# The output projection of a two-layer encoder step done by seven products of block sums, as the quad ahead of the MLP

## The reference

```python
    n = rms_norm(x, ln1_w)
    proj = n @ w_in
    q, k, v, g, gate_b, gate_c, hc = jnp.split(proj, SPLITS, axis=-1)
    ...
    ret_out = (jax.nn.silu(g.astype(jnp.float32)) * o).astype(x.dtype)
    ...
    conv_out = gate_b * z
    ...
    x = x + jnp.concatenate([ret_out, conv_out], axis=-1) @ w_out

    h2 = rms_norm(x, ln2_w)
    x = x + jnp.square(jax.nn.relu(h2 @ w_up)) @ w_down
```

## Time and profile before

| | us |
|---|---|
| median of 3 runs | 1404.87 (1402.94 to 1405.62) |
| the profiled execution, its own time | 1403.99 |
| its span, first to last instruction | 1402.0 |
| PE busy | 1381.7 (99%) |
| DVE busy | 897.2 (64%) |
| ACT busy | 594.9 (42%) |
| POOL busy | 166.0 (12%) |

### The profile page before, as it was taken

How to read it: one execution, slowest core, us unless ns; L and a number is a source line. 1 busy time by engine, 2 the same in 40 slices (tenths; PEclk the granted TensorE clock), 3 DMA queues, 4 the chain that set the end, 5 groups by cost and what they waited for, 6 DMA issues and landing times.

```text
span 1402.0 us, 21312 instructions
## 1 busy us (share of the span) xinstructions
PE 1381.7 (99%) x7750; PEld 1242.3 (89%) x7750; DVE 897.2 (64%) x1104; ACT 594.9 (42%) x712; POOL 166.0 (12%) x185
## 2 busy tenths in 40 slices
PE   8999999999999999999999999999999999999997
PEld 6888999889889899899878889998898998998986
DVE  6336515269976867868861474262788678688586
ACT  5211222157636446446533012231584464464563
POOL 2343200010000000000033431000100000000001
PEclk9999999999999999999999999999999999999999
DMA  7424212126454645455142242113345454544623
GB/s 274 136 76 122 83 50 73 55 105 156 88 153 121 150 98 149 140 116 159 31 134 102 91 121 68 61 62 120 76 129 142 110 158 124 121 121 121 151 61 105
DMA packets 91614, 158.18 MB, mean 113 GB/s; under 512 B 3892, under 2 KB 21428, under 8 KB 91512
## 3 DMA queue, kind: packets, MB, share of 16 engines
q1 hardware_dynamic: 74472, 123.18, 26.1%
q0 software_dynamic: 16896, 33.56, 14.1%
q10 hardware_dynamic: 144, 0.07, 0.0%
HBM read 149.38 MB, written 7.41 MB: 112 GB/s over the span
## 4 chain that ended last, share of the span: by engine, by line
PE 95%; DVE 1%; issue 1%; ACT 1%; DMA 0%; POOL 0%; SPq 0%; DVEq 0%; POOLq 0%; ACTq 0%
PE pair L776 27%; PE pair L615 23%; PE pair L832 21%; PE pair L625 12%; PE pair L845 6%; PE pair L665 2%; PE pair L703 1%; PE pair L710 1%; PE pair L684 1%; PE pair L688 1%; PE pair L693 1%; DMA w_raw<-in_w_in 0%; PE pair L696 0%; DVE ring L1738 0%; DVE x L1784 0%
## 5 line engine op out<-in xcount | busy, mean ns | idle before, releaser
L776 PE MATMUL pair<-mlp_in_hi,ring 128*128 128x320 f32 x1728 | 381.5, 309 | 0.0
L1104 ACT ACTIVATE ring<-raws 128x1024 fp32r<-128x1024 f32 x220 | 230.9, 1058 | 250.0 <-PE pair L832 129.8
L1738 DVE TENSOR_TENSOR ring<-raws,ring 128x1024 fp32r<-128x1024 f32 x220 | 267.1, 1221 | 103.0 <-ACT ring L1104 101.6
L832 PE MATMUL pair<-ring,a_ring 128*128 128x512 f32 x1344 | 312.1, 390 | 0.0
L832 PEld LDWEIGHTS pair<-ring,a_ring 128*128 128x128 f32 x1344 | 251.9, 188 | 52.5
L776 PEld LDWEIGHTS pair<-mlp_in_hi,ring 128*128 128x128 f32 x1728 | 289.1, 188 | 0.2
L776 PE MATMUL pair<-mlp_in_lo,ring 128*128 128x320 f32 x864 | 266.8, 309 | 0.0
L776 PEld LDWEIGHTS pair<-mlp_in_lo,ring 128*128 128x128 f32 x864 | 162.1, 188 | 0.2
L625 PE MATMUL pair<-norm_hi,ring 128*128 128x320 f32 x512 | 114.5, 310 | 0.0
L615 PE MATMUL pair<-ring,norm_hi 128*128 128x512 f32 x320 | 100.5, 395 | 2.7 <-DVE norm_lo L1502 2.6
L615 PE MATMUL pair<-pair_a,norm_hi 128*128 128x512 f32 x320 | 100.9, 397 | 0.0
(11 more groups left out here) (161 smaller groups left out, 1943.9 us busy)
## 6 DMA issues: line engine op xcount, KB each, us to landing
raws<-in_w_mlp_up SPq DMA_DIRECT2D x32, 1024.0 KB, 5.5
raws<-in_w_mlp_down SPq DMA_DIRECT2D x32, 1024.0 KB, 5.1
w_raw<-in_w_in SPq DMA_DIRECT2D x27, 1024.0 KB, 6.0
raws<-in_w_mlp_up POOLq DMA_DIRECT2D x16, 1024.0 KB, 9.0
raws<-in_w_mlp_down POOLq DMA_DIRECT2D x16, 1024.0 KB, 8.8
w_raw<-in_w_out SPq DMA_DIRECT2D x8, 1024.0 KB, 5.1
past_state<-in_state_ret SPq DMA_DIRECT2D x8, 512.0 KB, 4.4
out_ret_s<-past_state SPq DMA_DIRECT2D x8, 512.0 KB, 4.9
```

What stands on the lines that cost most here:

```text
L776: mm = pe.matmul(out[:, n, 0:HALF], item_half(item, h, a)[:, k, n * P:(n + 1) * P], mlp_in[i][c][:, k], start=(i in (B11, B21, SUM_1112, B ...
L832: mm = pe.matmul(out[:], a_item[:, a, 2 * h + k, pair * P:(pair + 1) * P], item_half(item, h, c)[:, k], start=(i in (B11, B21, SUM_1112) a ...
L1104: nc.scalar.activation(item_half(item, h, 0), raw_half(quad, RAW_OF[i], h), ACT.Copy).then_inc(half_hi.sem, 1)
L1738: nc.vector.tensor_tensor(item_half(item, h, 1), raw_half(quad, RAW_OF[i], h), f(item_half(item, h, 0)), ALU.subtract).then_inc(half_lo.se ...
```

## The change

O leaves the table of groups. The output projection becomes a down quad of its own, block number `OUT = -1`, ahead of the first MLP block: seven products with the four quarters of `w_out`, plus the sample's four. Its activations are the unsplit outputs in `hidden` (retention in the first half, z times B in the second), and `a_item_hi`, `a_item_lo`, `a_difference`, `mid_hi_of` and `sample_lo` split and sum them as in every down quad. All quads are numbered one higher. The transposes for the MLP's norm now stand between the pieces of that quad's last product (three tiles) and inside and behind the second half of the first up product (two tiles). The order of the tiles is the sample, then 0 to 3, and in the up quads the sample stands between the token halves (`MLP_PLACE`), so that tiles 0 and 1 and half of the sample make the first half. The squares go to a place of their own. Of the three input differences, two move to POOL.

```diff
-OUT_ORDER = [0, 1, 2, 3, SAMPLE]
+
+MLP_PLACE = {0: 0, 1: 1, SAMPLE: 2, 2: 3, 3: 4}
...
-          + [(s, ft, h) for s in "CHB" for ft in range(FT) for h in range(2)]
-          + [("O", dh, t) for dh in range(2) for t in OUT_ORDER])
+          + [(s, ft, h) for s in "CHB" for ft in range(FT) for h in range(2)])
...
-QUADS = 2 * NBLK
+QUADS = 2 * NBLK + 1
+OUT = -1
...
-                units(7, for_w_out, 0)
-                units(8, for_w_out, 1)
-
+                sp.wait_ge(group_done.sem, group_done.at(layer, STAGE_START[6]))
+                settle(sp)
+                for name in ("11", "12", "21", "22"):
+                    load_quarter(layer, 0, name)
...
+                            if b == 0 and i == B11 and h == 1:
+                                up_half(b, i, h, lambda: turn_tile(3))
+                                turn_tile(4)
+                            else:
+                                up_half(b, i, h)
...
+                                if b == OUT and i == SUM_ALL and (h, pair) != (1, 1):
+                                    turn_tile(2 * h + pair)
...
+                down(OUT)
                 for b in range(NBLK):
                     up(b)
                     down(b)
...
+                    if quad == 0:
+                        for t in range(NT):
+                            row_rstd(layer, NT, t)
+
+                        last = TURN["n2", NT - 1, 1]
+                        pool.wait_ge(turn_lo.sem, turn_lo.at(layer, split_turns_to(last)))
+                        nc.gpsimd.tensor_tensor(s2_raw[:], t_diff[:], t11[:], ALU.subtract).then_inc(s2_ready.sem, 1)
+                        nc.gpsimd.tensor_tensor(t21[:], t11[:], t21[:], ALU.subtract).then_inc(s3_ready.sem, 1)
...
                 def up(b):
-                    q, item = 2 * b, 2 * b * PRODUCTS
-                    if b:
-                        for p in range(2):
-                            add_to_x(b - 1, SUM_ALL, p)
-                    else:
-                        weight_half(1, 0)
+                    q, item = 2 * b + 1, up_item(b, 0)
+                    for p in range(2):
+                        add_to_x(b - 1, SUM_ALL, p)
+                    if b == 0:
+                        weight_half(item, 1)
+                        normalise(layer, NT, 3, ORDER[3], 32)
+                        normalise(layer, NT, 4, ORDER[4], 32)
+                        weight_half(item + 1, 0)
+                        read_turn_lo(layer, ("n2", 3, 1))
+                        weight_half(item + 1, 1)
+                        read_turn_lo(layer, ("n2", 4, 1))
                         weight_sum(q, SUM_1112, 0)
-                    weight_half(item + 1, 1)
-                    if b == 0:
+                        in_diff_lo_of(0)
+                        weight_half(item + 2, 0)
+                        hidden_sum(b, B21, 0)
                         weight_sum(q, SUM_1112, 1)
-                        read_turn_lo(layer, ("n2", NT - 2, 1))
-                    weight_half(item + 2, 0)
-                    if b == 0:
-                        read_turn_lo(layer, ("n2", NT - 1, 1))
-                    weight_sum(q, SUM_111222, 0)
-                    if b == 0:
-                        in_diff_lo_of(0)
-                        hidden_sum(b, B21, 0)
-                        in_difference(1)
+                        hidden_sum(b, B21, 1)
                         weight_half(item + 2, 1)
-                        hidden_sum(b, B21, 1)
-                        weight_sum(q, SUM_111222, 1)
+                        weight_sum(q, SUM_111222, 0)
                         in_diff_lo_of(1)
                         weight_half(item + 3, 0)
-                        in_difference(0)
+                        weight_sum(q, SUM_111222, 1)
...
+                    if b == OUT:
+                        add_to_x(b, B22, 0)
+                        normalise(layer, NT, 0, ORDER[0], 32)
+                        add_to_x(b, B22, 1)
+                        weight_half(item + 7, 0)
+                        normalise(layer, NT, 1, ORDER[1], 32)
+                        read_tile_lo(0)
+                        normalise(layer, NT, 2, ORDER[2], 32)
+                        read_tile_lo(1)
+                        read_tile_lo(2)
+                        return
```

More of the change, by code:

```diff
@@ L72 @@
 TURN = {x: n for n, x in enumerate(TURNS)}
[L73 to L74 removed]
+SPLIT_TURNS = [n for n, x in enumerate(TURNS) if x[0] == "n1"
+               or (x[0] == "n2" and (ORDER[x[1]] not in (2, 3) or x[2] == 1))]
 def split_turns_to(n):
@@ L317, in n2_parts @@
         def n2_parts(tile):
-            first = tile * P
+            first = MLP_PLACE[tile] * P
             out = []
@@ L773, in up_half @@
                     for n in range(2):
+                        if n and between:
+                            between()
                         for k in range(4):
@@ L812, in wait_banks, with turn_tile @@
                             layer, b * len(C_SUMS) + C_SUMS.index((read, h)) + 1))
+                def turn_tile(p):
+                    for c in range(2):
+                        turn(layer, ("n2", p, c))
                 def up(b):
@@ L907, in square @@
             def square(layer, base, p, tile):
-                if p >= 2:
-                    turns = TURN["n1" if base == 0 else "n2", p - 2, 1]
-                    act.wait_ge(turned.sem, turned.at(layer, turns + 1))
-                nc.scalar.activation(xn[:, p % 2], x[:, tile], ACT.Square,
+                if p >= 2 and base == 0:
+                    act.wait_ge(turned.sem, turned.at(layer, TURN["n1", p - 2, 1] + 1))
+                elif p >= 2:
+                    act.wait_ge(squares.sem, squares.at(layer, NT + p - 1))
+                nc.scalar.activation((squares_2 if base else xn)[:, p % 2], x[:, tile], ACT.Square,
                                      accum_out=sums[:, p:p + 1]).then_inc(squares.sem, 1)
@@ L1160, in mid_hi_of @@
                         act.wait_ge(layer_out.sem, layer_out.at(layer, 48))
-                    nc.scalar.activation(sample_mid[n][0][:], h51 if n == 0 else h52, ACT.Copy).then_inc(mid_hi.sem, 1)
+                    nc.scalar.activation(sample_mid[n][0][:], sample_of(b, int(n > 0)), ACT.Copy).then_inc(mid_hi.sem, 1)
                 def a_item_hi(b, i):
-                    n = b * PRODUCTS + i
-                    if i in (B11, B21, SUM_ALL):
+                    n = a_to(b, i) - 1
+                    if b == OUT and i in (B21, SUM_ALL):
+                        act.wait_ge(vector_read.sem, vector_read.at(
+                            layer, MIX_VECTOR.index(GROUP["B", FT - 1, int(i == SUM_ALL)]) + 1))
+                    elif b == OUT and i == B11:
+                        act.wait_ge(small_read.sem, small_read.at(layer, len(SMALLS)))
+                    elif i in (B11, B21, SUM_ALL):
@@ L1194, in in_diff_hi_of @@
-                    nc.scalar.activation(dst[:], src[:], ACT.Copy).then_inc(in_diff_hi.sem, 1)
+                    else:
+                        ready = (s2_ready, s3_ready, s4_ready)[n - 1]
+                        act.wait_ge(ready.sem, ready.at(layer, 1))
+                        dst, src = ((mlp_in[SUM_111222][0], s2_raw), (mlp_in[SUM_1222][0], t21),
+                                    (mlp_in[B22][0], s4_raw))[n - 1]
+                    nc.scalar.activation(dst[:], src[:], ACT.Copy, scale=1.0 if n else -1.0).then_inc(in_diff_hi.sem, 1)
@@ L1265, in down @@
                         weight_half(item + 8, 0)
-                out_square(0)
-                out_square(1)
-                for h in range(2):
-                    weight_half(0, h)
-                for p in range(2, NT):
-                    for c in range(2):
-                        read_turn(layer, ("n2", p - 2, c))
-                    out_square(p)
+                a_item_hi(OUT, B11)
+                weight_half(0, 0)
+                first_tap(2)
+                weight_half(0, 1)
+                first_tap(3)
+                a_item_hi(OUT, B21)
+                weight_half(1, 0)
+                mid_hi_of(OUT, 1)
+                mid_hi_of(OUT, 0)
+                down(OUT)
                 for b in range(NBLK):
```

490 lines of the change are left out of this document (244 added, 246 removed).

## The result

The changed kernel takes 1408.86 us (median of 6 runs, 1407.2 to 1409.65) against 1404.03 for the kernel before on the same chip (6 runs): ratio 1.0032, interval 1.0019 to 1.0045. It is **slower, by 4.8 us**, where "no change" at 1404.6 was forecast; the time lies just inside the upper end of the range. Its profiled execution has a span of 1407.1 us.

The account below looks back on a forecast made before the run. TensorE, busy 99% of the span, was taken as the bound. Per layer 5.46 + 2.3 - 1.6 - 0.8 - 5.3 = 0.1 us gained, 0.2 in all, from 1404.87 to 1404.6 us; range 1393 to 1409.

Parts of the forecast that it names:

- no change: Whole kernel: 1404.6 us, within 0.2% (2.8 us) of the kernel before; chance of landing within 0.36.
- Removed, 5.46 + 2.3: Output projection and old seam: 5.46 us less TensorE work and 2.3 us of waits gone per layer.
- Ahead of and inside the new quad, and in the regular blocks, nothing: Projection quad and eight MLP blocks: no added wait, costed at zero, up to 1 us allowed ahead of the quad.
- Transposes, 1.6 + 0.8: New seam: 1.6 us added wait for three tiles in the last product, 0.8 for the other two, per layer.
- Subtractions, +5.3: New seam: POOL's two subtractions, 2.9 us each, hold DVE up; 5.3 us added wait before the third product per layer.
- Rival 1: New seam: POOL and DVE run side by side, 5.8 us gained per layer, 1393.2 us; chance 0.20.
- rival 2: New seam: only one subtraction hurts, 2 to 3 us gained per layer, 1398.5 to 1401 us; chance 0.14.
- rival 3: New seam: POOL's subtractions longer, over 0.2% slower from 3.7 us each, 1411 us at 4.5; chance 0.14.
- Rival 4: New quad: gaps because the second product's conv half or weights come late, 1 to 2 us per layer; chance 0.05.
- Behind it everything is later by the same amount, with no second wait: After the wait before the third product: later work only shifts; POOL's accumulating load still has 2 us to spare.
- Slower: Whole kernel: more than 0.2% slower than the kernel before; chance 0.24.

Follow-up runs that it names:

- e2: Changed kernel with both subtractions left out, their readers reading t11 instead (wrong numbers): 1397.21 us against 1404.37 for the kernel before.
- e9: Changed kernel with 20 unused 128x128 matmuls put into TensorE's wait before the first up block's third product: 1405.20 us; kernel before 1403.75.
- e3: Changed kernel with both subtractions still on POOL, but started only after the second product's hidden sums: 1409.44 us against 1404.37 for the kernel before.
- e4: Kernel before, with TensorE waiting for 2, 3 and 4 small POOL operations before the sixth up product of blocks 1, 2, 3: span 1443.9 us.
- e8: Kernel before, with TensorE waiting for 1, 2 and 2 small POOL operations before the sixth up product of blocks 1, 2, 3: span 1430.1 us.
- e6: Changed kernel with DVE and ACT operations around the seam reordered as in e5, subtractions on POOL: 1399.32 us; kernel before 1403.18.
- e5: Changed kernel with both subtractions on DVE and DVE and ACT operations around the seam reordered: 1393.19 us; kernel before 1403.18.
- e7: Changed kernel with POOL's two subtractions replaced by same-size copies (wrong numbers): 1397.52 us against 1403.18 for the kernel before.
- e1: Changed kernel with both subtractions moved from POOL to DVE, right behind the first input remainder: 1402.11 us against 1404.37 for the kernel before.

## Why the prediction was wrong

The sum was 0.1 us gained per layer; the trace has 1.9 and 2.8 lost, 4.9 us more than forecast in both together. By its steps:

- **Removed, 5.46 + 2.3: right.** The seam without the subtractions (e2) is 4.46 us shorter; by the sum, less the transposes' measured 3.15 below, it should be 4.6.
- **Ahead of and inside the new quad, and in the regular blocks, nothing: right.** No gap, and 98.47 us.
- **Transposes, 1.6 + 0.8: 0.75 too small.** (The addends of the first give 10.9, not 11.05, and so 1.5.) From 246.59 to 300.25, where the up quad starts, it is 53.66 us for 49.14 of products and 2.6 of transposes, 1.9 lost; from there to the wait (317.33) 17.1 for 14.1 and 1.75, 1.25 lost. Idle time is only 0.95 and 0.94 of it; the rest is PE's busy time at the changes between products and transposes, which I had priced at nothing.
- **Subtractions, +5.3: right.** 2.8 us each of their own (2.9 taken), DVE held up for their whole length (5.16 measured, 5.5 forecast), 4.9 us of wait. At full clock they cost 5.2 us per layer (e9's seam of 111.23 less e2's 106.05). Rival 1 (side by side), rival 2 and rival 3 (3.7 us and more) are out: DVE was held up, by both, and POOL's rows of 3.89 and 4.12 us hold 1 us and more of waiting (2.94 and 2.89 in e3). Rival 4 didn't occur.
- **"Behind it everything is later by the same amount, with no second wait": this sentence failed.** What follows a wait is not PE's work at PE's pace. The clock fell behind it, in both layers, and cost 1.2 and 2.1 us (e9 against the change). The sum has no term for it.

Added up: 2 x 0.75 more at the transposes, 2 x 0.1 less at the subtractions, 3.3 for the clock, 4.6 us of the 4.9; the other 0.3 are the difference between 4.46 and 4.6 above, twice, and stay open. The times themselves, 1408.86 and 1404.6, are only 4.3 apart, because the forecast started from a median of 1404.87 and six runs of the kernel before gave 1404.03: that part of the nearness is luck. With the clock kept up the kernel takes 1405.2 (e9, against 1403.75 before), "no change". The trace of before had no wait of PE above 1.7 us between 244 and 1050, and so no row of a fall; but a wait of 5.3 us that a forecast adds is itself outside what the rows cover, and there I gave no bound for the matmuls behind it. "Slower" had 0.24 of the chances, none of it for this.

## What to carry to other kernels

A wait of TensorE has two prices, its length and the half clock behind it: in these runs nothing up to 2.1 us, in one of two at 2.5, in nine of ten from 3.0 to 3.5 (the six of e4 and e8, and four at the end of layer 0, below), and in all ten from 4.4 up; a fall between products of the MLP cost 1.2 to 2.8 us. So two short waits can be cheaper than one long one (e6's 1.89 and 1.34 us had no fall behind them), and what gets a wait from 3 us or more below 2 gains more than its length. Handing DVE's SBUF-to-SBUF work to POOL takes nothing off DVE while both are busy: POOL's 2.8 us stood against DVE's 1.4; what pays is DVE's own order, with the work put where its first reader needs it (e5 beats the kernel before by 10 us, with the changed kernel's operations and both subtractions back on DVE).

## What the runs showed of the hardware beyond that

- Exclusion works over the whole instruction in both directions (POOL's first subtraction stood still for the 1.06 us that DVE's weight sum had left, DVE's remainder for POOL's 2.8), though the kernel before had shown the one direction with 0.30 us only the earlier trace rows.
- A fall is no property of the program alone. At the end of layer 0, in code that no run changes, PE's wait for DVE was 0.65 us in e3, 1.37 in e5, 1.62 in the change, 1.69 in the kernel before, 2.10 in e7, and 3.04 to 3.34 in e2, e4, e6 and e8; behind the last four the clock fell (the next two matmuls took 1.12 to 1.22 us instead of 0.73). The wait hangs on a stretch in which DVE stands idle, for 3.37 us in e3 and 5.74 in e4, and waits for nothing that the profile shows; what that is stays open.
- The clock can also be half in the first 15 us. In the changed kernel it is 0.55 in the row below and 1.00 in the kernel before. The three other executions with such a row (e1, e3, e9) also begin the projection at 246.7 to 246.8, but e6, without one, at 246.90; so that the 0.5 us of later start lie there is likely and not shown.

```profile
12.00:15.00 3.00, 3.00 (x9) 2.34 (x8) 2.33 (x4) 1.47 (x4) 1.64 (x3) 0.55 1.04 410
```
